# Indexer scores: the longest row block is weighted on ScalarE and added up on GpSimd

## The reference

```
qi = rope(qi.reshape(B, S, 16, 64), pos) * 64 ** -0.5
ki = rope(ki[:, :, None, :], pos)[:, :, 0, :]
wi = wi * 16 ** -0.5
logits = einsum('bqhd,bkd->bqhk', qi, ki)          # 16 indexer heads
score  = einsum('bqh,bqhk->bqk', wi, relu(logits)) # sum over the heads
score  = where(kpos <= qpos, score, -inf)
sel    = top_k(score, 256)
```

## Time and profile before

| | us |
|---|---|
| median of 3 runs | 3623.88 |
| lowest to highest | 3623.08 to 3627.99 |
| the profiled execution, its own time | 3628.1 |
| its span | 3626.3 |
| TensorE busy | 3270.4 (90%) |
| VectorE busy | 1818.7 (50%) |
| ScalarE busy | 1278.6 (35%) |
| GpSimd busy | 821.7 (23%) |

### The profile page before, as it was taken

How to read it: one execution, slowest core, us unless ns; L and a number is a source line. 1 busy time by engine, 2 the same in 40 slices (tenths; PEclk the granted TensorE clock), 3 DMA queues, 4 the chain that set the end, 5 groups by cost and what they waited for, 6 DMA issues and landing times. The chain is left out here.

```text
span 3626.3 us, 45156 instructions
## 1 busy us (share of the span) xinstructions
PE 3270.4 (90%) x15622; PEld 2684.2 (74%) x15622; DVE 1818.7 (50%) x3077; ACT 1278.6 (35%) x2732; POOL 821.7 (23%) x509
## 2 busy tenths in 40 slices
PE   8778986969889999999988998799888999999988
PEld 6556875857667888888866886677677888888866
DVE  2398994748424444444442431688524444444342
ACT  3364424747423222222232211677513221222231
POOL 2332264345211000000031441666211000000030
PEclk9899998989989999999999999899998999999999
DMA  4203222212212111111021223222112111111021
GB/s 131 53 16 104 93 90 82 47 41 59 82 47 82 47 35 58 46 35 58 0 76 38 93 98 128 52 49 55 53 42 58 58 46 49 46 44 58 0 76 47
DMA packets 268629, 214.78 MB, mean 59 GB/s; under 512 B 95164, under 2 KB 220908, under 8 KB 268524
## 3 DMA queue, kind: packets, MB, share of 16 engines
q1 hardware_dynamic: 268524, 213.43, 19.9%
HBM read 170.93 MB, written 41.94 MB: 59 GB/s over the span
## 5 line engine op out<-in xcount | busy, mean ns | idle before, releaser
L67 PE MATMUL l0in_acc<-l0in_w_lo,l0h_hi 128*128 128x512 f32 x384 | 151.9, 395 | 25.0 <-POOL l0in_w_lo L1581 25.0
L1655 DVE TENSOR_SCALAR_CACHE_REDUCE k_x<-k_x,l0in_cand 128x384 bf16<-128x384 f32 (+1 forms) x186 | 163.7, 942 | 1.1
L1860 DVE SCALAR_TENSOR_TENSOR l1ff_c<-l1ff_g,l1ff_cw,l1ff_c 128x512 f32<-128x512 f32 x44 | 33.1, 752 | 252.9 <-ACT l1ff_c L1775 252.9
L1860 DVE SCALAR_TENSOR_TENSOR l0ff_c<-l0ff_g,l0ff_cw,l0ff_c 128x512 f32<-128x512 f32 x44 | 33.1, 751 | 251.3 <-ACT l0ff_c L1775 251.3
L131 POOL MEMSET l1pg_mhalf<- 128x8 f32 x1 | 0.1, 105 | 701.1 <-POOLq L106 701.1
L131 POOL MEMSET l0pg_mhalf<- 128x8 f32 x1 | 0.1, 104 | 701.0 <-POOLq L106 701.0
L1881 DVE TENSOR_TENSOR k_x<-l1ff_d,k_x 128x512 f32<-128x512 f32 x176 | 118.0, 689 | 81.0 <-PE l1ff_d L69 81.0
L1881 DVE TENSOR_TENSOR k_x<-l0ff_d,k_x 128x512 f32<-128x512 f32 x176 | 118.0, 689 | 81.0 <-PE l0ff_d L69 81.0
L67 PE MATMUL l1in_acc<-l1in_w_lo,l1h_hi 128*128 128x512 f32 x384 | 150.5, 392 | 5.6 <-POOL l1in_w_lo L467 5.5
L69 PE MATMUL l0in_acc<-l0in_w_hi,l0h_hi 128*128 128x512 f32 x384 | 151.1, 394 | 0.0
L68 PE MATMUL l0in_acc<-l0in_w_hi,l0h_lo 128*128 128x512 f32 x384 | 151.1, 393 | 0.0
(11 more groups left out here) (442 smaller groups left out, 9760.4 us busy)
## 6 DMA issues: line engine op xcount, KB each, us to landing
l0in_raw<-in_w_in_even SPq DMA_DIRECT2D x24, 512.0 KB, 4.0
l1in_raw<-in_w_in_odd SPq DMA_DIRECT2D x24, 512.0 KB, 3.7
l0ff_raw_g<-in_w_gate SPq DMA_DIRECT2D x22, 512.0 KB, 4.1
l0ff_raw_u<-in_w_up SPq DMA_DIRECT2D x22, 512.0 KB, 5.3
l0ff_raw_d<-in_w_down SPq DMA_DIRECT2D x22, 512.0 KB, 4.9
l1ff_raw_g<-in_w_gate SPq DMA_DIRECT2D x22, 512.0 KB, 4.0
l1ff_raw_u<-in_w_up SPq DMA_DIRECT2D x22, 512.0 KB, 5.2
l1ff_raw_d<-in_w_down SPq DMA_DIRECT2D x22, 512.0 KB, 4.8
```

The source lines that it names most:

```text
L67: pe.matmul(out, a_hi, b_lo, start=start, stop=False)
L1655: tick(dve.tensor_scalar(hits[:, cols], score[:, cols], cand[:, i:i + 1].bitcast(F32), 0.0, ALU.is_ge, ALU.add, accum_out=cnt[:, i:i + 1]))
L1860: dve.scalar_tensor_tensor(c[:, half, :], g[:, at - 1:at + 511], cw[:, 1, bass.ds(blk, 1)], c[:, half, :], ALU.mult, ALU.add).then_inc(con ...
```

## The change

Two things are changed in `indexer_stage`.

First, the 1024 block (`LAST`) is no longer summed by VectorE. ScalarE rectifies it into a buffer of its own, `r_last`, multiplies it there by the head's weight in a second instruction (Copy with a per-partition scale, in place), and GpSimd adds `r_last` to the scores (`last_row`). The buffer ring `r` is now counted over the five other blocks of a head. ScalarE waits with the rectified block for GpSimd's addition of the head before. On GpSimd the rotation of head h+2 stands ahead of the addition of head h.

Second, TensorE's scores wait on `relu_done`, which ScalarE raises when a block is rectified, in place of `s_free`, which VectorE raised.

```
-                for t in range(T0, NT):          # VectorE
-                    u = h * NSEL + (t - T0)
+                for t in range(T0, LAST):
                     cols = score[:, sel_at(t):sel_at(t + 1)]
-                    dve.wait_ge(relu_done, u + 1)
-                    dve.sem_inc(s_free, 1)
-                    dve.scalar_tensor_tensor(cols, r[:, t % 2, 0:(t + 1) * P], wi[:, t, bass.ds(h, 1)], cols,
+                    dve.wait_ge(relu_done, h * NSEL + (t - T0 + 3))
+                    dve.scalar_tensor_tensor(cols, r[:, (b * ROWS + t) % 2, 0:(t + 1) * P], wi[:, t, bass.ds(h, 1)], cols,
                                              ALU.mult, ALU.add).then_inc(acc_done, 1)
...
+                    act.wait_ge(s_done, h * NSEL + (t - T0) + 1)          # ScalarE
+                    if t == LAST:
+                        act.wait_ge(last_acc, h + 1)
+                        act.activation(r_last[:], ps_s[:, t % 2, :], ACT.Relu).then_inc(relu_done, 1)
+                        act.wait_ge(relu_done, h * NSEL + (NSEL + 2))
+                        act.activation(r_last[:], r_last[:], ACT.Copy, scale=wi[:, LAST, bass.ds(h, 1)]).then_inc(weighed, 1)
+                    else:
+                        act.wait_ge(acc_done, h * ROWS + (t - T0) + 1)
+                        act.activation(r[:, (b * ROWS + t) % 2, 0:(t + 1) * P], ps_s[:, t % 2, 0:(t + 1) * P], ACT.Relu).then_inc(relu_done, 1)
...
+            def last_row(h):                                              # GpSimd
+                cols = score[:, sel_at(LAST):sel_at(LAST + 1)]
+                pool.wait_ge(weighed, h + 1)
+                pool.tensor_tensor(cols, cols, r_last[:], ALU.add).then_inc(last_acc, 1)
+                pool.wait_ge(last_acc, h + 2)
...
+            queries(0, 0)
+            queries(1, 1)
+            with pool.Fori(0, LOOP) as j:
                 for b in range(2):
+                    queries(2 * j + b + 2, b)
+                    last_row(2 * j + b)
+            for b in range(2):
+                last_row(2 * LOOP + b)
...
-                    pe.wait_ge(s_free, u + 1)                             # TensorE
+                    pe.wait_ge(relu_done, u + 1)
```

More of the change, by code:

```diff
@@ L1286, in indexer_stage @@
         raw_in = [st.sem(f"raw_in{b}") for b in range(2)]
-        (dup_in, pool_step, raw_free, stage_ready, stage_free, turned, hi_done, lo_done, s_done, relu_done, acc_done, zeroed, s_free) = (
+        (dup_in, pool_step, raw_free, stage_ready, stage_free, turned, hi_done, lo_done, s_done, relu_done, acc_done, last_acc, zeroed, weighed) = (
             st.sem(n) for n in ("dup_in", "pool_step", "raw_free", "stage_ready", "stage_free", "turned", "hi_done",
-                                "lo_done", "s_done", "relu_done", "acc_done", "zeroed", "s_free"))
+                                "lo_done", "s_done", "relu_done", "acc_done", "last_acc", "zeroed", "weighed"))
         seen = st.sem("seen")
+        LAST = NT - 1
+        ROWS = NSEL - 1
         block = st.block()
@@ L1332, in rotate, with queries @@
                 before(4)
+            def queries(h, b):
+                pool.wait_ge(raw_in[b], (h - b) * 8 + 16)
+                pool.wait_ge(stage_free, h + 1)
+                rotate(stage[:, b, 0:NSEL, :], raw[:, b, :, :], T0, NSEL,
+                       lambda k: pool.wait_ge(pool_step, h * 4 + (4 + k)))
+                pool.sem_inc(raw_free, 1)
+                pool.sem_inc(stage_ready, 1)
+            def last_row(h):
[3 more added lines that the diff above has]
+                pool.wait_ge(last_acc, h + 2)
             pool.memset(score, 0.0).then_inc(zeroed, 1)
@@ L1337, in _ @@
             pool.sem_inc(stage_ready, 1)
-            with pool.Fori(0, IDXH // 2) as j:
+            pool.sem_inc(last_acc, 1)
+            queries(0, 0)
+            queries(1, 1)
+            with pool.Fori(0, LOOP) as j:
                 for b in range(2):
[L1340 to L1346, removed]
+                    queries(2 * j + b + 2, b)
+                    last_row(2 * j + b)
+            for b in range(2):
+                last_row(2 * LOOP + b)
         halves = [(0, 4), (4, NSEL)]
@@ L1358, in body @@
                 for t in range(T0, NT):
-                    u = h * NSEL + (t - T0)
-                    act.wait_ge(s_done, u + 1)
-                    act.wait_ge(acc_done, u + 1)
-                    act.activation(r[:, t % 2, 0:(t + 1) * P], ps_s[:, t % 2, 0:(t + 1) * P], ACT.Relu).then_inc(relu_done, 1)
+                    act.wait_ge(s_done, h * NSEL + (t - T0) + 1)
[7 more added lines that the diff above has]
+                        act.activation(r[:, (b * ROWS + t) % 2, 0:(t + 1) * P], ps_s[:, t % 2, 0:(t + 1) * P], ACT.Relu).then_inc(relu_done, 1)
                     if t - T0 < 2 and more:
                         hi_part(h + 1, 1 - b, t - T0)
+            act.sem_inc(relu_done, 2)
             for n in range(2):
@@ L1370, in _ @@
                 hi_part(0, 0, n)
+            act.wait_ge(zeroed, 2)
             heads(act, body)
```

3 lines of the change are left out of this document (1 added, 2 removed).

## The result

| | before | after |
|---|---|---|
| median, us | 3623.93 (6 runs) | 3654.36 (6 runs) |
| lowest to highest | 3623.08 to 3632.21 | 3651.01 to 3655.43 |
| ratio to before | | 1.0077, 95% interval 1.0066 to 1.0087 |
| the profiled execution, its span | 3628.1, 3626.3 | 3654.7, 3652.9 |
| indexer stage ends (GpSimd's first operation of the next stage) | 275.95 | 306.14 |

The change makes the kernel slower by 30.4 us. The forecast was 20.7 us slower, and the measured time lies 3.4 us above the range. The sign and the mechanism were right; a third of the loss was not in the sum.

What follows compares the result with a forecast made beforehand. VectorE, busy 45.3 of 48 us, was taken as the bound. Thirteen heads at 9.17, one at 9.00, the last 7.51 and a final addition 2.37 ended the stage at 296.38: +20.7 on 3623.9, 3644.6 us; range 3634 to 3651.

Steps and rivals of the forecast that it cites:

- The exclusion: VectorE sums and GpSimd operations with two SBUF inputs exclude each other; each new addition holds VectorE's sums 2.18 us.
- The weighting: ScalarE's new 128x1024 multiplication by the head's weight, 16 in the stage: 1.15 us each, ends 1.03 and 1.24.
- the addition: GpSimd's new 128x1024 addition, 16 in the stage: 2.37 us each, always issued before VectorE's next 384 sum.
- Rival A: No exclusion of this kind, VectorE gets relief: 7.38 us a head, -5.8 us, 3618.1; chance 0.05.
- rival B: The 384 sum gets in before GpSimd's addition, which hides behind `lo_part`: 8.67 us a head, 3637.6; chance 0.05.
- The third rotation step or the 640 sum: Undecided order of GpSimd's step and VectorE's sum: 9.34 us a head if the step goes first, otherwise 9.00; middle 9.17 taken.
- first addition starts: GpSimd's first addition in the indexer stage, forecast to start at 158.29, with little changed up to there.
- the head without a rotation: The one head, after thirteen with a rotation beside them, that has none: 9.00 us.
- last head: The stage's final head, without `lo_part`, its 512 and 640 sums taking 1.55: 7.51 us.
- What I cost at nothing: TensorE's scores on `relu_done`, ScalarE's and GpSimd's new waits, and SyncE's loads: no time added.
- rival C: TensorE's clock falls as longer heads idle it: up to 43 us more or nothing, half of it 3666; chance 0.03.
- signs of being wrong: 384 sum under 1 us, head under 8 us, weighting over 1.3 us, or granted clock under 1.00 in the steady part.

Runs made afterwards that it cites:

- the later addition: Changed kernel with two extra unread matmuls per score block, GpSimd's addition also waiting for VectorE's 384 sum of the next head, except the last: 3653.9 us, one run.
- busy TensorE: Changed kernel with two more 512-column matmuls behind each block's scores, into a PSUM bank nobody reads: 3649.58 us, ratio to before 1.0066.
- The short addition: Changed kernel with GpSimd's addition cut to 128 of 1024 columns, the rest left out, weighting kept whole: 3623.23 us, one run.
- the second pair of profiles: Changed kernel and kernel before, nothing edited, each profiled once more: 3656.5 and 3626.51 us; stage ends at 303.46 and 275.68.

## Why the prediction was right in direction and short in size

*The exclusion* (sums held for GpSimd's duration less 0.19, the one issued first goes first) held in each row and was undone by moving an input to PSUM. *The weighting* was put at 1.15 us and took 1.150 in the mean of 16; *the addition* 2.37 at 2.373. The addition 0.07 behind the weighting and ahead of the 384 sum: so it was. *Rival A* fell with the first 384 sum of 2.35, *rival B* with the later addition, which gained nothing. Three readings in the working are off without touching the forecast: VectorE's "97% share" is 94% (45.31 of 48 us), rival A's terms make 7.37 and not 7.38, and 0.39 - 0.06 is 0.33.

*The third rotation step or the 640 sum:* the step goes first. The prediction took the middle, 9.17; full-clock heads are 9.23 with GpSimd's loop written out. That is 13 x 0.06 = 0.8 us too little.

The sum ended the stage's last addition at 296.38; it ended at 303.33 + 2.34 = 305.67. The 9.3 us between come apart as follows, each by the trace or a run:

| term | forecast | found | us |
|---|---|---|---|
| first addition starts | 158.29 | 160.31 | 2.0 |
| 13 heads: order at the 640 sum | 9.17 | 9.23 | 0.8 |
| 13 heads: end of GpSimd's loop | not in the sum | 9.23 to 9.36 | 1.7 |
| 13 heads: TensorE's clock | not in the sum | 9.36 to 9.57 | 2.7 |
| the head without a rotation | 9.00 | 9.23 | 0.2 |
| last head | 7.51 | 9.45 | 1.9 |

**The step that failed** is the last of the working, "What I cost at nothing": TensorE "isn't on the loop (6.0 us busy a head)". That was a reading of busy time at full clock, and the prediction knew the condition, since it made rival C of it, but gave C a chance of 0.03 and a price of all or nothing. Its own list of signs of being wrong had a granted clock under 1.00 in the steady part, and this sign came. What came was a part of C. In the steady part the clock spent some of its time at the half level, ScalarE waited 0.2 to 0.4 us for TensorE in 7 of 9 heads, and the heads with a busy TensorE put the price at 2.7 us. The last head has no turned queries and the shortest way through VectorE, so TensorE has the least cover there; it took 1.94 us more than forecast.

Of these 1.94 us, 0.96 went with the busy TensorE. The other 0.98 came at full clock, with waits of 0.39 and 0.47 us for TensorE, but there TensorE had two extra matmuls ahead of each block. The short addition has neither them nor a lower clock, and ScalarE still waited 0.50 and 0.30 us for TensorE in its last head. So the cover was thin even at full clock; what the changed kernel's last head would take there without the extra matmuls isn't measured.

The head before the last went from 9.23 to 8.87 with the busy TensorE, 0.36 us (the forecast's 9.00 lies between). With it the busy TensorE gave back 4.0 us in all. That is the lower clock's part of the 9.3 as far as it was measured, and, since the extra matmuls cost time themselves, rather its least. The start's 2.0 us lie behind a TensorE at half clock in both kernels (0.50 from 140 to 150 us), differ between executions of one kernel (158.01 and 160.31) and shouldn't be laid to the change.

The other thing left out was the end of GpSimd's loop. Before, nothing was behind it: GpSimd was idle 4 us a head. The change queues a rotation behind the addition, and with that the 0.5 us between two turns moves a rotation step onto VectorE's 512 sum. The rows of before couldn't price it, but in the changed code the loop's end plainly lies between the addition and the rotation.

Two things stay open. Why the clock falls in the change and not before is shown only as far as this: TensorE's weight loads wait up to 1.5 us at a time (before up to 0.9), its busy time in the 48 us is 33.7 where it was 36.2 although part of it ran slower, and keeping it busy holds the clock at 1.00. Which of the two, the longer gaps or the smaller share, matters wasn't told apart. And 30.4 us in the medians are 2.6 more than the stage's 27.8 us in the second pair of profiles and as much as its 30.2 in the first; the rest of the kernel is 4.5 us apart in the two profiled executions of the changed kernel, and I can't place these.

## What to carry to other kernels

Before an elementwise operation is moved from VectorE to GpSimd, look at what VectorE runs beside it: if that has two SBUF inputs and GpSimd's operation reads SBUF too, nearly GpSimd's whole duration can come back on VectorE, here 2.2 us for a sum of 1.2. Find it out from the kernel before, in one head read row by row: two durations that are odd (0.61 and 1.37 for the same sum) said it. The cure was no rearrangement in time, which only moved the hold; it was to leave one input in PSUM, which, with a third buffer, made the kernel before 13.6 us faster and gave the changed one back its 30. And where a change lengthens a loop, don't take TensorE as covered because it is three quarters busy at full clock, as it was here: price it once at half clock, in the shortest head too, and give that a real chance.

## What the runs showed of the hardware

A GpSimd `tensor_tensor` of 128x1024 with both inputs in SBUF made a sum of 0.61 us take 2.35; a memset of 1.93 us and a sum from PSUM beside the same addition left it at 0.62. GpSimd's loop took 0.65 us from the last operation of one turn to the first of the next, where neighbours within a turn stood 0.16 apart, and 0.08 when written out. Extra matmuls that nobody reads held the changed kernel's granted clock at 1.00, where it had been 0.89, and made its stage 4.0 us shorter between first and last addition; they gave the kernel before nothing and made its heads 0.08 to 0.7 us longer.
